# Moving the low halves of most weight pieces from GpSimd to VectorE in a two-layer diffusion backbone step

## The reference, cut to what matters

```
h = rmsnorm(x, norm1_g) * (1 + sc1) + sh1
proj = h @ w_in                        # inputs of three mixers, and the gates
o_gla, o_conv, o_diff = gated linear attention, convolution, differential attention
merged = ga * (o_gla @ wb[:512]) + gb * (o_conv @ wb[512:1024]) + gc * (o_diff @ wb[1024:])
x = x + g1 * (merged @ w_out)
h2 = rmsnorm(x, norm2_g) * (1 + sc2) + sh2
a, b = split(h2 @ w_ffn_in);  x = x + g2 * ((silu(a) * b) @ w_ffn_out)
```

## Time and profile before

| what | value |
|---|---|
| median of 3 runs (their range) | 1651.69 us (1645.64 to 1657.51) |
| the profiled execution, its own time | 1658.13 us |
| its span, first to last instruction | 1656.2 us |
| mean granted TensorE clock | 0.963 |
| PE busy | 1520.1 us, 92% |
| POOL busy (288 subtractions) | 735.5 us, mean 2556 ns |
| ACT, DVE busy | 577.7 us, 758.7 us |
| w_raw loads on the one queue | 512 KB each, median 3.3 to 3.7 us from issue to landing |

### The profile page before, as it was taken

One profiled execution on the slowest core, in us unless ns is written; L12 is line 12 of the kernel. 1 busy time (PEld: TensorE's weight loads), 2 busy tenths in 40 slices (PEclk: granted clock), 3 DMA queues, 4 the chain that ended last, 5 costly groups with the idle time before them and its releaser, 6 DMA issues.

```text
span 1656.2 us, 22476 instructions
## 1 busy us (share of the span) xinstructions
PE 1520.1 (92%) x9085; PEld 1399.0 (84%) x9085; DVE 758.7 (46%) x1048; ACT 577.7 (35%) x763; POOL 735.7 (44%) x292
## 2 busy tenths in 40 slices
PE   5799799998998999999989979889899899999998
PEld 2688788878898799999968779788789879999997
DVE  3358999244474411210041889971445642212102
ACT  2323232244453433333232233223446243333321
POOL 1353455323346455555534443532334545555551
PEclk9899799999999999999989989999999999999999
DMA  8852222322253355554337422232222533444341
GB/s 317 284 188 87 66 75 84 86 73 71 81 186 123 119 168 190 171 194 132 125 104 254 128 81 73 64 89 83 64 77 77 204 115 115 128 127 127 118 125 63
DMA packets 161262, 208.65 MB, mean 126 GB/s; under 512 B 9228, under 2 KB 135176, under 8 KB 161160
## 3 DMA queue, kind: packets, MB, share of 16 engines
q1 hardware_dynamic: 161160, 207.22, 39.1%
HBM read 204.05 MB, written 3.15 MB: 125 GB/s over the span
## 4 chain that ended last, share of the span: by engine, by line
PE 61%; DVE 25%; ACT 5%; DMA 4%; issue 3%; POOL 2%; SPq 1%; DVEq 0%; ACTq 0%; POOLq 0%
PE ps L596 17%; PE ps L597 17%; PE ps L598 17%; DVE conv_acc L1373 9%; DMA w_raw<-in_w_out_dram 2%; PE ps L548 2%; POOL w_lo L519 2%; PE ps L563 2%; DVE fac L1502 1%; DVE attn L1513 1%; DVE t L1337 1%; PE ps L690 1%; ACT w_hi L1040 1%; DVE prefix L1453 1%; DVE mx L1602 1%
## 5 line engine op out<-in xcount | busy, mean ns | idle before, releaser
L519 POOL TENSOR_TENSOR w_lo<-w_raw,w_hi 128x1024 fp32r<-128x1024 f32 x288 | 735.5, 2556 | 891.7 <-ACT w_hi L1040 698.6
L596 PE MATMUL ps<-h_hi,w_hi 128*128 128x384 f32 x1600 | 562.5, 352 | 31.8 <-DVE h_lo L1343 19.4
L597 PE MATMUL ps<-h_lo,w_hi 128*128 128x384 f32 x1600 | 545.2, 341 | 0.0
L598 PE MATMUL ps<-h_hi,w_lo 128*128 128x384 f32 x1600 | 545.0, 341 | 0.0
L1040 ACT ACTIVATE w_hi<-w_raw 128x1024 fp32r<-128x1024 f32 x200 | 210.8, 1056 | 536.8 <-PE ps L598 425.3
L596 PEld LDWEIGHTS ps<-h_hi,w_hi 128*128 128x128 f32 x1600 | 308.3, 193 | 62.7 <-issue 33.5
L597 PEld LDWEIGHTS ps<-h_lo,w_hi 128*128 128x128 f32 x1600 | 308.7, 193 | 1.8
L598 PEld LDWEIGHTS ps<-h_hi,w_lo 128*128 128x128 f32 x1600 | 308.0, 193 | 0.0
L1373 DVE SCALAR_TENSOR_TENSOR conv_acc<-conv_in,cw,conv_acc 128x399 f32<-128x399 f32 x240 | 183.3, 836 | 0.1
L1254 ACT ACTIVATE w_hi<-w_raw 128x1024 fp32r<-128x1024 f32 x88 | 93.3, 1060 | 244.7 <-PE ps L598 227.5
L1657 DVE TENSOR_TENSOR sq<-sq,ps 128x768 f32<-128x768 f32 x22 | 21.0, 954 | 273.3 <-PE ps L598 273.3
(11 more groups left out here) (226 smaller groups left out, 1766.8 us busy)
## 6 DMA issues: line engine op xcount, KB each, us to landing
w_raw<-in_w_in_dram SPq DMA_DIRECT2D x112, 512.0 KB, 3.6
w_raw<-in_w_ffn_in_dram SPq DMA_DIRECT2D x88, 512.0 KB, 3.5
mod_late<-in_w_mod_dram SPq DMA_DIRECT2D x64, 512.0 KB, 5.9
w_raw<-in_w_ffn_out_dram SPq DMA_DIRECT2D x44, 512.0 KB, 3.7
mod_early<-in_w_mod_dram SPq DMA_DIRECT2D x32, 512.0 KB, 5.3
w_raw<-in_w_branch_dram SPq DMA_DIRECT2D x24, 512.0 KB, 3.3
w_raw<-in_w_out_dram SPq DMA_DIRECT2D x16, 512.0 KB, 3.4
out_dram<-stage SPq DMA_DIRECT2D x6, 256.0 KB, 2.3
```

Of the source, the lines that this page charges most:

```text
L519: nc.gpsimd.tensor_tensor(m["w_lo"][:, j], m["w_raw"][:, j % RAW], m["w_hi"][:, j].bitcast(F32), ALU.subtract).then_inc(lo_ready.sem, 1)
L596: mm(out, hi[:, at:at + P], rhs[0][:, k, :], start=start, stop=False)
L597: mm(out, hi[:, at:at + P], rhs[1][:, k, :], start=False, stop=False)
L598: ins = mm(out, lo[:, at:at + P], rhs[0][:, k, :], start=False, stop=stop)
```

## The change

VectorE makes the low halves of pieces 62 to 143 of each layer (82 of 144), GpSimd those of pieces 0 to 61. GpSimd counts its own on the semaphore `lo_p`, VectorE on `lo_v`; `low_done` picks the right one for whoever waits. VectorE's subtractions (the new helper `low`) are set into its list by hand: one behind each gate multiply of the branch stage (piece n + 4 behind piece n), then in the output stage, one within the second norm, four in each round of the hidden layer, and the rest ahead of the last additions to `x`.

```diff
--- before.py
+++ after.py
@@ -75,6 +75,8 @@
 BR0, WO0, FI0, FO0 = N_IN, N_IN + N_BR, N_IN + N_BR + N_WO, N_IN + N_BR + N_WO + N_FI
 PIECES = FO0 + N_FO
 assert PIECES % SPL == 0 and PIECES % RAW == 0
+
+VLO = BR0 + 4
@@ -223,7 +225,8 @@
         raw_full = [signal(f"raw_full{i}", 16 * PIECES // RAW) for i in range(RAW)]
         hi_ready = signal("hi_ready", PIECES, RAW)
-        lo_ready = signal("lo_ready", PIECES, RAW)
+        lo_p = signal("lo_p", VLO, RAW)
+        lo_v = signal("lo_v", PIECES - VLO)
         piece_used = signal("piece_used", PIECES, SPL)
         late_full = [signal(f"late_full{i}") for i in range(LATE)]
@@ -337,6 +340,12 @@
         fin_p = signal("fin_p")
         y_out = signal("y_out")
+        def low_done(layer, s):
+
+            if s < 0 and layer:
+                layer, s = layer - 1, s + PIECES
+            return lo_p.at(layer, s + 1) if s < VLO else lo_v.at(layer, s - VLO + 1)
+
         def keys_of(q):
             return P if q == 0 else T
@@ -412,7 +421,7 @@
                 def piece(s, src):
                     sp.wait_ge(*hi_ready.at(l, s - RAW + 1))
-                    sp.wait_ge(*lo_ready.at(l, s - RAW + 1))
+                    sp.wait_ge(*low_done(l, s - RAW))
                     k, n = src.shape[0] // P, src.shape[1]
                     sp.dma_start(m["w_raw"][:, s % RAW, 0:k * n].rearrange("p (k n) -> p k n", k=k),
                                  src.rearrange("(k p) n -> p k n", p=P)).then_inc(raw_full[s % RAW].sem, 16)
@@ -511,13 +520,13 @@
         @block.gpsimd
         def _(pool):
-            pool.sem_inc(lo_ready.sem, RAW)
-            for g in range(DEPTH * PIECES // 4):
-                for j in range(4):
-                    pool.wait_ge(raw_full[j % RAW].sem, g * (16 * 4 // RAW) + 16 * (j // RAW + 1))
-                    pool.wait_ge(hi_ready.sem, g * 4 + (j + 1 + RAW))
-                    nc.gpsimd.tensor_tensor(m["w_lo"][:, j], m["w_raw"][:, j % RAW], m["w_hi"][:, j].bitcast(F32),
-                                            ALU.subtract).then_inc(lo_ready.sem, 1)
+            pool.sem_inc(lo_p.sem, RAW)
+            for l in range(DEPTH):
+                for s in range(VLO):
+                    pool.wait_ge(*raw_full[s % RAW].at(l, 16 * (s // RAW + 1)))
+                    pool.wait_ge(*hi_ready.at(l, s + 1))
+                    nc.gpsimd.tensor_tensor(m["w_lo"][:, s % SPL], m["w_raw"][:, s % RAW], m["w_hi"][:, s % SPL].bitcast(F32),
+                                            ALU.subtract).then_inc(lo_p.sem, 1)
         @block.tensor
@@ -601,7 +610,7 @@
                 def split(s):
                     pe.wait_ge(*hi_ready.at(l, s + 1))
-                    pe.wait_ge(*lo_ready.at(l, s + 1))
+                    pe.wait_ge(*low_done(l, s))
                 h = (m["h_hi"], m["h_lo"])
@@ -954,8 +963,7 @@
                     for half_chunk in range(4):
                         half, part_b = half_chunk % 2, half_chunk // 2
                         s = FI0 + half_chunk
-                        pe.wait_ge(hi_ready.sem, l * PIECES + i * 4 + (s + 1 + RAW))
-                        pe.wait_ge(lo_ready.sem, l * PIECES + i * 4 + (s + 1 + RAW))
+                        split(s + 4 * i)
                         if half_chunk == 0:
                             pe.wait_ge(silu_a.sem, l * PAIRS + (i + 1))
                         if half_chunk == 2:
@@ -1330,6 +1338,12 @@
                 SEGS = ((0, slice(0, TP)), (1, slice(TP, T)))
+                def low(s):
+
+                    dve.wait_ge(*hi_ready.at(l, s + 1))
+                    v.tensor_tensor(m["w_lo"][:, s % SPL], m["w_raw"][:, s % RAW], m["w_hi"][:, s % SPL].bitcast(F32),
+                                    ALU.subtract).then_inc(lo_v.sem, 1)
+
                 def norm_t(which, k):
                     if k >= 2:
                         dve.wait_ge(*h_lo_ready.at(l, 2 * (KD * which + k - 1)))
@@ -1351,6 +1365,8 @@
                     for k in range(1, KD):
                         norm_t(which, k)
                         norm_low(which, k - 1)
+                        if which and k == 4:
+                            low(FI0 + 3)
                     norm_low(which, KD - 1)
                 def add_to_x(tile, src, gate):
@@ -1626,6 +1642,7 @@
                     dve.wait_ge(*piece_used.at(l, BR0 + n + 1))
                     dve.wait_ge(*gsig.at(l, 1 + mc // 2 if b == 0 else {2: 3, 1: 4}[b]))
                     done(v.tensor_tensor(g, g, pair[n % 4], ALU.mult), gated)
+                    low(BR0 + n + 4)
                     if n == 0:
                         dve.wait_ge(*conv_hi_a.at(l, 1))
                         done(v.tensor_tensor(m["conv_lo"][:], m["conv_z"][:], m["conv_hi"][:].bitcast(F32), ALU.subtract),
@@ -1637,10 +1654,14 @@
                         dve.wait_ge(*merged_a.at(l, mc + 1))
                         hi = m["h_hi"][:, 2 * mc:2 * mc + 2, :].bitcast(F32)
                         done(v.tensor_tensor(m["h_lo"][:, 2 * mc:2 * mc + 2, :], a, hi, ALU.subtract), merged_v)
+                low(WO0 + 4)
+                low(WO0 + 5)
                 for cc in range(4):
                     for i in range(2):
                         dve.wait_ge(*(piece_used.at(l, WO0 + OUT_ORDER.index((cc, 1)) + 1) if i else tile_done.at(l, cc + 1)))
                         add_to_x(2 * cc + i, pair[cc % 2][:, i, :], 16)
+                    for n in ((6,), (7,), (8, 9, 10), ())[cc]:
+                        low(WO0 + n)
                 modulated_norm(1)
                 for i in range(PAIRS):
@@ -1652,18 +1673,26 @@
                         mod_final(40, 48)
                     if l + 1 < DEPTH and i in (5, 9):
                         mod_take(l + 1, i // 4 - 1)
+                    low(FI0 + 4 * i + 4)
+                    low(FI0 + 4 * i + 5)
                     dve.wait_ge(*silu_a.at(l, i + 1))
                     dve.wait_ge(*piece_used.at(l, FI0 + 4 * i + 4))
                     v.tensor_tensor(m["sq"][:], m["sq"][:], pair[1], ALU.mult).then_inc(u_v.sem, 1)
+                    low(FI0 + 4 * i + 6)
+                    low(FI0 + 4 * i + 7)
                     dve.wait_ge(*uhi_a.at(l, i + 1))
                     v.tensor_tensor(m["act_lo"][:, 2 * i:2 * i + 2, :], m["sq"][:],
                                     m["act_hi"][:, 2 * i:2 * i + 2, :].bitcast(F32), ALU.subtract).then_inc(ulo_v.sem, 1)
                     if l + 1 < DEPTH and i in (5, 9):
                         mod_put(l + 1, i // 4 - 1)
                 for g in range(2):
+                    for n in ((range(4, 14)), (range(15, N_FO)))[g]:
+                        low(FO0 + n)
                     for i in range(4):
                         dve.wait_ge(*(piece_used.at(l, FO0 + 11 * (g + 1)) if i == 3 else tile_done.at(l, 5 + 3 * g + i)))
                         add_to_x(4 * g + i, ps[:, 4 * g + i, 0:T], 40)
+                    if g == 0:
+                        low(FO0 + 14)
             dve.wait_ge(fin_a.sem, 2)
             for k in range(KD):
```

## The result

The changed kernel takes **1656.82 us** (median of 20 runs, 1652.4 to 1666.1), the kernel before beside it 1651.02 us (20 runs, 1643.85 to 1660.46): 5.8 us longer, a ratio of 1.0037 with an interval of 1.0022 to 1.0052. The forecast was 1660.2 us. The two profiled executions, 1658.17 us now and 1658.13 us before, don't show this difference: that of before lies 7 us above its median. So the account is made stage by stage.

What follows compares the result with a forecast made beforehand. TensorE was taken as the bound (busy 1520.1 of 1656.2 us), with weight halves on the path in the output stage. 2 x (0.3 + 1.95 + 1.25) + 1.5 = 8.5 us gave 1660.2 us on the median, range 1645 to 1671.

Steps and rivals of the forecast that it cites:

- behind piece 72: 0: Rest of the output stage after piece 72: no change, since it waits for TensorE.
- The price of the subtraction: One 1024-element subtraction on VectorE: 1.22 us, estimated between two neighbouring sizes, against 2.40 us on GpSimd.
- Hidden layer: Hidden layer and last pieces (82 to 143): 0, covered by the lead of four pieces.
- The load of piece 70: +0.3 us: Branch stage: VectorE's list delays piece 69's load, and piece 70 lands a fixed time after its issue; +0.3 us per layer.
- Start of the branch stage: 0: Before piece 62: a subtraction delays the convolution's low half by 1.22 us less 0.4, taken up by later idle time; 0.
- From the landing to piece 72: +1.95: Output stage, from piece 70's landing: additions queue behind subtractions that wait for loads; +1.95 us per layer.
- Norm: +1.25: Second norm: one subtraction with its gap ahead of the fifth tile delays the end of piece 79; +1.25 us per layer.
- Clock: +1.5 in the second layer: Piece 72 after longer idle time runs partly at 1.2 GHz: +1.5 us, second layer; upper end once more in each layer.
- The sum: All terms over both layers: 8.5 us slower, lower ends 4.2, with more clock loss 11.5; forecast 1660.2 us.
- The faster one: Rival: chain subtractions cost 1.22 instead of 2.40 us if n = 8's addition ends before L + 1 (L: piece 70's landing); 1641 us, chance 0.13.
- VectorE as the bound in the hidden layer: Rival: hidden-layer loads wait for subtractions that wait for the product, one microsecond missing in each of 22 rounds; 1682 us, chance 0.07.
- a subtraction of 2.40 us: Rival: the subtraction is no cheaper on VectorE, costing 8.3 us more per layer in norm and load chain; 1677 us, chance 0.04.

Runs made afterwards that it cites:

- the run with it alone: Against the changed kernel, VectorE makes only the low halves of pieces 82 to 143, GpSimd 0 to 81: 1650.12 us, ratio 0.9987 to the kernel before.
- The run with the additions first: Changed kernel with the branch stage's subtractions moved behind the addition of their piece: 1646.90 us, ratio 0.9977 to the kernel before.
- both positions mended: Changed kernel with piece 81's subtraction ahead of the second norm and the branch stage's subtractions behind the additions: 1646.97 us, ratio 0.9971 to the kernel before.
- the loads brought forward: Loads of pieces 70 to 73 issued ahead of seven `mod_late` loads: kernel before 1658.08 us, changed kernel 1657.26; with both subtraction moves too, 1640.78.

## Why the prediction was near, and what was wrong in it

The mechanism in VectorE's list held; one step failed, by 1.5 us per layer, and the terms that hang on loads and on the clock were off in single layers. Changes against before in the two profiled executions, in us (the length of a piece is from the start of its first matmul to the end of its last):

| step, per layer | predicted | first layer | second layer |
|---|---|---|---|
| end of piece 61 to the issue of piece 69's load | +0.3 | -1.23 | -1.29 |
| from there to the landing of piece 70 | 0 | -0.82 | -1.35 |
| landing of piece 70 to the start of piece 72 | +1.95 | +1.73 | +0.31 |
| length of piece 72 (clock) | 0, +1.5 | +0.95 | +1.54 |
| fifth tile of the second norm | +1.25 | +1.03 | +1.00 |
| the stretch | +3.5, +5.0 | +1.66 | +0.21 |

The five rows add up to the stretch, so nothing else in it changed: "behind piece 72: 0" was right.

**The price of the subtraction**: 1.22 us, as taken from the line between two neighbours. **Hidden layer**: 0, right, and shown by the run with it alone.

**The load of piece 70: +0.3 us** is the step that failed. The walk itself was near: from the end of the high half of piece 65 to the end of the subtraction of piece 67 it gave 9.81 us, and the trace has 9.51 (467.71 to 477.22). But I began it at the time that the high half of 65 had before (471.24), and that had moved: it now ends 7.02 us after piece 61, and ended 8.25 us after it before. That the landing of piece 70 comes a fixed time after that issue was wrong too: it took 15.41 and 16.58 us before, 14.59 and 15.23 us now.

**Start of the branch stage: 0** was wrong for the same reason as the starting time of that walk: I counted the subtraction that VectorE gets there, 1.22 us, and not that the lock goes with GpSimd's subtraction of piece 62. I had named that lock for the additions and `act_lo`, whose long cases stand in the earlier trace rows; I didn't ask which other VectorE instructions GpSimd's subtractions met. The Trainium skill's rule (SBUF — State Buffer, section "Who interferes with whom") speaks of every VectorE instruction with two SBUF inputs; `gg` with 1.84 against 0.62 us agrees with it, though it ended 0.41 us after the subtraction, where a block for the whole instruction would leave its full 0.62.

**From the landing to piece 72: +1.95**. In the first layer 17.95 us, predicted 18.15. In the second 16.20, predicted 17.8: the load of piece 73 took 3.29 us and not the 4.63 that I carried over from before; with that load it would be 17.5. The run with the additions first shows that the place in the list is the cause.

**Norm: +1.25** measured 1.0. **Clock: +1.5 in the second layer**: right, piece 72 pays it there now (granted clock 0.60 from 1320 to 1324 us), 5.97 against 4.43 us. That piece 70 pays no longer (4.40 against 5.99 us) gives nothing back, since piece 72 waits for `h_lo` either way. In the first layer piece 72 grew from 5.97 to 6.92 us, part of the upper end that I had allowed.

**The sum.** As they stand, the two profiled stretches differ by 1.9 us, the medians by 5.8 us (3.6 to 8.6 by the interval). With the landing of piece 70 and the load of piece 73 as they were before, the stretch would be 2.4 us longer in the first layer and 2.9 in the second, 5.3 us together, and the forecast without the missed gain of 1.5 us per layer would have been 5.5. That these figures agree so closely is luck more than evidence. The load of piece 73 was mostly short where the subtractions stand ahead of the additions (last section), so a part of what is set back here may belong to the change. And outside the stretch the executions differ by several us: the second layer up to piece 61 takes 419.3 to 422.7 us in the four profiles with the additions first and 421.8 to 427.2 us in the nine others, with equal instruction lists for these pieces. Where the other 3.9 us between the medians lie can't be told from single profiles and stays open.

**The rivals.** The faster one had its deciding point right: the addition of n = 8 does not end within 1 us of the landing (it ends 3.3 us after it), and it is the position that decides. With both positions mended the gain is 4.8 us by the ratio, less than half of that rival's 10.7; the loads are still on the chain there (11.20 us for piece 70 and 4.61 us for piece 73 in the first layer). VectorE as the bound in the hidden layer and a subtraction of 2.40 us are excluded by the trace.

## What to carry to other kernels

Moving an operation to an engine that does it in half the time is worth what its new place in that engine's list is worth: put behind a wait for a load and ahead of an addition that was ready, and between two tiles of a norm, it lost 0.4%, and behind that addition, with the other subtraction taken out of the norm, it gained 0.3%. For each operation that leaves an engine, list what the other engine ran at the same time, over the whole program and not only where the change was made: what it was blocking speeds up too. A load brought forward pushes others back on the same queue, so follow those to the instruction that waits for them before counting the gain.

## What the runs showed of the hardware

- One subtraction on GpSimd that overlaps `gg` stretches it from 0.62 to 1.84 us, in every profile where GpSimd makes piece 62, and in none where VectorE does. `gg` began 0.98 us after the subtraction and ended 0.41 us after it.
- Loads at the same place of the same queue take unlike times. In the eight kernels with the loads in their first order, the load of piece 73 took 3.26 to 5.51 us. In the four that issue it 0.2 to 0.3 us before piece 72 lands (the kernel before, the hidden layer alone, and the two with the additions first) it took 4.61 to 5.51 us in both layers; in the four that issue it 1.6 to 1.8 us after that landing it took 3.26 to 3.43 us six times, and 5.05 and 5.33 us. With the loads brought forward, four loads issued 0.2 to 0.3 us before the landing took 3.32 to 3.54 us, so that overlap alone isn't the reason; what is was not found. Where piece 72 waits for this load, that is up to 2.2 us per layer.
- After an idle time of 2.56 us before it, piece 72 took 4.43 us (first layer of the kernel with both moves), after 2.70 us 5.97 us (its second layer), and after the 5.98 us of the changed kernel 6.92 us, with a granted clock of 0.53 from 508 to 515 us, that is, mostly at 1.2 GHz. So 0.14 us more of waiting came with 1.54 us more of work. The idle time alone doesn't set this price: in the kernel where GpSimd makes piece 62 again, piece 72 took 7.24 us after 4.19 us in the first layer, and 5.97 us after 4.18 us in the second.
